# A hybrid decoder layer on one core: the decode sequences of gated linear attention in row and column groups, and decode attention with its two kv heads in turn

## The reference, cut to what matters

```python
    def step(S, xs):
        qd_i, kdec_i, v_i, bl_i = xs
        o_i = jnp.einsum('bhtd,bhde->bhte', qd_i, S)
        S = jnp.exp(bl_i)[:, :, 0, :, None] * S + jnp.einsum('bhsd,bhse->bhde', kdec_i, v_i)
        return S, o_i
```

## Time and profile before

| | before |
|---|---|
| median of three runs | 2471.78 us |
| the profiled execution | 2467.32 us |
| its span | 2465.5 us |
| TensorE busy (weight loads) | 2346.9 us, 95% (2182.4, 89%) |
| VectorE, ScalarE, GpSimd busy | 63%, 37%, 10% |
| mean granted clock of TensorE | 0.983 |
| chain that ended last | TensorE 91%, DMA 3%, VectorE 2%, issue 2%, ScalarE 1% |

### The profile page before, as it was taken

How to read it: one execution, slowest core, us unless ns; L and a number is a source line. 1 busy time by engine, 2 the same in 40 slices (tenths; PEclk the granted TensorE clock), 3 DMA queues, 4 the chain that set the end, 5 groups by cost and what they waited for, 6 DMA issues and landing times.

```text
span 2465.5 us, 44142 instructions
## 1 busy us (share of the span) xinstructions
PE 2346.9 (95%) x18537; PEld 2182.4 (89%) x18537; DVE 1553.5 (63%) x2236; ACT 921.7 (37%) x1324; POOL 238.7 (10%) x285
## 2 busy tenths in 40 slices
PE   5689999999999899899999999999999989999996
PEld 1179888788787799899999999999999989999996
DVE  0342552323232422588888888888888788888898
ACT  2122442323232322544444444444444433333343
POOL 3150140000000111200000000000000211011131
PEclk9989999999999999999999999999999999999998
DMA  9955465555553434214434433443344586365562
GB/s 339 342 184 175 154 157 190 188 181 188 171 192 121 160 110 127 103 69 167 150 123 162 163 118 126 164 166 135 135 167 166 207 301 212 132 228 203 172 212 95
DMA packets 190949, 422.41 MB, mean 171 GB/s; under 512 B 14564, under 2 KB 116756, under 8 KB 188704
## 3 DMA queue, kind: packets, MB, share of 16 engines
q1 hardware_dynamic: 171072, 341.35, 40.4%
q0 software_dynamic: 17088, 73.78, 8.6%
q10 hardware_dynamic: 2592, 4.46, 0.5%
HBM read 365.45 MB, written 54.08 MB: 170 GB/s over the span
## 4 chain that ended last, share of the span: by engine, by line
PE 91%; DMA 3%; DVE 2%; issue 2%; ACT 1%; SPq 0%; POOL 0%; DVEq 0%; POOLq 0%; ACTq 0%
PE PJ L2290 27%; PE PS L2290 27%; PE PJ L1924 25%; DMA AR<-in_weights 3%; PE PJ L1877 2%; PE PJ L1867 1%; PE PJ L2255 1%; PE PS L2150 1%; PE PS L2181 1%; PE PS L2255 1%; PE PS L2174 1%; PE PJ L1889 1%; PE PJ L2232 1%; DVE X L1844 0%; PE PS L2153 0%
## 5 line engine op out<-in xcount | busy, mean ns | idle before, releaser
L2290 PE MATMUL PS<-HS,WO 128*128 128x272 f32 x5376 | 684.2, 289 | 10.3 <-issue 9.5
L2290 PEld LDWEIGHTS PS<-HS,WO 128*128 128x128 f32 x5376 | 679.4, 188 | 11.9 <-issue 11.9
L2290 PE MATMUL PJ<-HS,WO 128*128 128x272 f32 x5376 | 680.6, 288 | 0.0
L2290 PEld LDWEIGHTS PJ<-HS,WO 128*128 128x128 f32 x5376 | 677.3, 188 | 0.0
L1100 ACT ACTIVATE WO<-GR 128x1024 fp32r<-128x1024 f32 (+1 forms) x462 | 477.0, 1033 | 508.5 <-PE PS L2290 243.6
L1619 DVE TENSOR_TENSOR WO<-GR,WO 128x1024 fp32r<-128x1024 f32 (+1 forms) x462 | 556.2, 1204 | 117.6 <-ACT WO L1100 117.5
L1924 PE MATMUL PJ<-HH,WH 128*128 128x272 f32 x1568 | 348.1, 304 | 20.7 <-issue 7.9
L1924 PE MATMUL PJ<-HL,WH 128*128 128x272 f32 x1568 | 327.7, 291 | 0.0
L1924 PE MATMUL PJ<-HH,WL 128*128 128x272 f32 x1568 | 327.5, 291 | 0.0
L1259 DVE TENSOR_TENSOR WL<-RW,WH 128x1024 fp32r<-128x1024 f32 x102 | 129.4, 1273 | 285.5 <-ACT WH L839 285.2
L1924 PEld LDWEIGHTS PJ<-HH,WH 128*128 128x128 f32 x1568 | 248.7, 191 | 55.2 <-issue 43.3
(11 more groups left out here) (308 smaller groups left out, 1846.3 us busy)
## 6 DMA issues: line engine op xcount, KB each, us to landing
GR<-in_weights SPq DMA_DIRECT2D x264, 512.0 KB, 6.7
AR<-in_weights SPq DMA_DIRECT2D x256, 256.0 KB, 4.5
RW<-in_weights SPq DMA_DIRECT2D x102, 512.0 KB, 4.4
HS<-act_parts POOLq DMA_DIRECT2D x91, 544.0 KB, 5.9
act_parts<-SQ SPq DMA_DIRECT2D x40, 952.0 KB, 7.0
AR<-in_weights SPq DMA_DIRECT2D x64, 512.0 KB, 5.3
MIX<-in_xT SPq DMA_DIRECT2D x1, 4352.0 KB, 16.7
X<-in_xT POOLq DMA_DIRECT2D x4, 1088.0 KB, 10.1
```

The costliest lines, as they stand in the source:

```text
L2290: mm = e.matmul(out, w[part], HS[:, HS_AT[QUARTER[i]], y, (2 * first + k) % (KT // 2), :], start=OPENS[i] and k == 0 and x == 0, stop=k == ...
```

## The change

GLA, decode part. A span of 32 tokens that starts at sequence 2j (`windows`, `scol(2 * j)`) is given to column group and row group j = 0 to 3, so its first eight tokens are those of sequences 2j and 2j + 1. `turn_windows` replaces the 32-column transposes of keys and values by four matmuls with the identity into the four partition quarters. `dec_outs`, at k=6 of gg0, makes all decode outputs with 12 matmuls: for each j the masked queries of its two sequences times their states, and ATD times values, into free columns of a PJ bank. ScalarE copies them to OTD (128 rows, of each group the first eight count) in gg0, squares them into OTS with the blocks, and takes the root ahead of the adaLN rows of gg1. `seq_pair(n)`, at k=7, 9, 12 and 14 of gg1, makes two state updates from two row groups, into two PSUM banks. VectorE applies them in the new order; the last four come after the reciprocal and the scaling of OT. KDM is made by two products with a per-row mask DR, which is loaded by four small DMAs on GpSimd ahead of the caches. `o_turn` transposes OTD 128 wide, and `mix_head` picks eight columns of each 32.

Decode attention. `dec_scores` and `dec_values` run the same matmuls in another order: the kv head is the inner loop, so neighbouring matmuls belong to different halves of the array.

```diff
-    KDM = sb("KDM", [32, DEC_B, P], at=en_at)
+    KDM = sb("KDM", [P, 2, P], at=en_at)
...
-    OTD = sb("OTD", [32, DV])
+    OTD = sb("OTD", [P, DV])
...
-    ATD = sb("ATD", [32, 32])
+    ATD = sb("ATD", [P, 64])
...
+    def windows(t):
+x = decode(t)
+return bass.AP(x.tensor, x.offset, [x.ap[0], [2 * DEC_T, 4], [1, 32]], runtime_checks=x.runtime_checks,
+               dep_tracking_offset=x.dep_tracking_offset)
+    def dec_out(m):
+return PJ[:, 2 * (m + 1).mod(2) + 1, DV:2 * DV]
...
+lo, up = CST["dec_rows"]
+for j in range(4):
+    g.dma_start(DR[32 * j:32 * j + 32, :], ins["consts"][0:32, lo:up]).then_inc(S["masks_in"], 16)
...
-        a.activation(GVT[0:32, NB, P * e:P * e + P], PS[0:32, 1, 0:P], ACT.Copy).then_inc(S["gv_by_token"], 1)
+        a.activation(GVT[:, NB, P * e:P * e + P], PS[:, 1, 0:P], ACT.Copy).then_inc(S["gv_by_token"], 1)
...
+    a.wait_ge(S["dec_out_mm"], h + 1)
+    a.activation(OTD[:, :], dec_out(m), ACT.Copy).then_inc(S["out_sq"], 1)
...
+    a.wait_ge(S["out_sq"], (NB + 2) * h + 1)
+    a.activation(OTS[:, :], OTD[:, :], ACT.Square, accum_out=VR[:, 0, NB:NB + 1]).then_inc(S["out_sq"], 1)
+    a.wait_ge(S["out_sq"], (NB + 2) * (h + 1))
+    a.activation(VR[:, 1, :], VR[:, 0, :], ACT.Sqrt, bias=eps, scale=1.0 / DV).then_inc(S["norm_rms"], 1)
...
-    a.wait_ge(S["dec_out_mm"], h + 1)
-    a.activation(OTD[:, :], PS[0:32, 3, 0:DV], ACT.Square, accum_out=VR[0:32, 0, NB:NB + 1])\
-        .then_inc(S["out_sq"], 1)
-    a.wait_ge(S["out_sq"], (NB + 1) * (h + 1))
-    a.activation(VR[:, 1, :], VR[:, 0, :], ACT.Sqrt, bias=eps, scale=1.0 / DV).then_inc(S["norm_rms"], 1)
     a.wait_ge(S["norm_r"], h + 1)
     for b in range(NB // 2):
         a.activation(OT[:, b, :], o_block(b), ACT.Copy, scale=VR[:, 2, b:b + 1]).then_inc(S["out_scaled_a"], 1)
-    a.activation(OTD[:, :], PS[0:32, 3, 0:DV], ACT.Copy, scale=VR[0:32, 2, NB:NB + 1])\
-        .then_inc(S["out_scaled_a"], 1)
+    a.activation(OTD[:, :], OTD[:, :], ACT.Copy, scale=VR[:, 2, NB:NB + 1]).then_inc(S["out_scaled_a"], 1)
...
+        d.scalar_tensor_tensor(out=decode(tile).rearrange("p (j t) -> p j t", j=4),
+                               in0=PS[:, 2, P * e:P * e + P].rearrange("p (j c) -> p j c", j=4)[:, :, 0:8],
+                               scalar=gain, in1=decode(GG[e][:, :]).rearrange("p (j t) -> p j t", j=4),
+                               op0=ALU.mult, op1=ALU.mult)\
...
+    cols = cst("dec_cols")[:, 0:64].rearrange("p (g c) -> p g c", g=2).unsqueeze(2).broadcast_to([P, 2, 4, 32])
+    d.tensor_tensor(QDM[:, :, :].rearrange("p (g j) c -> p g j c", g=2), windows(GQ[:, :]).unsqueeze(1).broadcast_to([P, 2, 4, 32]), cols, ALU.mult)\
+        .then_inc(S["q_by_seq"], 1)
...
+    d.wait_ge(S["masks_in"], 48 + 64)
+    for n in range(2):
+        mm = d.tensor_scalar(KDM[:, n, :], KDT[:, NB, :], DR[:, n:n + 1], None, ALU.mult)
+    mm.then_inc(S["k_by_seq"], 1)
...
-    for b in range(DEC_B):
-        if b == 4:
-            lo(v + (1 + LEAD))
-        if b == 5:
-            head_mod("gg1")
+    def seq_update(x):
+        b = 2 * (x % 4) + x // 4
...
+        d.wait_ge(S["seq_mm"], DEC_B * h + x + 1)
         d.scalar_tensor_tensor(out=SD[:, b, :], in0=SD[:, b, :], scalar=EB[:, last:last + 1],
-                               in1=PS[:, 2, 0:DV], op0=ALU.mult, op1=ALU.add)\
-            .then_inc(S["seq_up"], 1)
-
+                               in1=chunk_up(x), op0=ALU.mult, op1=ALU.add).then_inc(S["seq_up"], 1)
...
+    for b in range(2):
+        seq_update(b)
+    lo(v + (1 + LEAD))
+    for b in range(2, 4):
+        seq_update(b)
+    head_mod("gg1")
...
     d.wait_ge(S["norm_rms"], h + 1)
     d.reciprocal(VR[:, 2, :], VR[:, 1, :]).then_inc(S["norm_r"], 1)
     d.wait_ge(S["norm_r"], h + 1)
     for b in range(NB // 2, NB):
         d.tensor_scalar(OT[:, b, :], o_block(b), VR[:, 2, b:b + 1], None, ALU.mult)\
             .then_inc(S["out_scaled_d"], 1)
+    for b in range(4, DEC_B):
+        seq_update(b)
...
-    for kv in range(KVH):
-        rows = slice(HD * kv, HD * kv + HD)
+    for new in range(2):
         for b in range(DEC_B):
-            out = PS[32 * (b % 4):32 * (b % 4) + 32, kv, 160 * (b // 4):160 * (b // 4) + 160]
-            e.matmul(out[:, 0:WIN], QS[rows, b, :], KC[rows, b, :], start=True, stop=True)
-            mm = e.matmul(out[:, WIN:160], QS[rows, b, :], decode(KTT[rows, :]), start=True, stop=True)
-        mm.then_inc(S["dec_scores"], 1)
+            for kv in range(KVH):
+                rows = slice(HD * kv, HD * kv + HD)
+                out = PS[32 * (b % 4):32 * (b % 4) + 32, kv, 160 * (b // 4):160 * (b // 4) + 160]
+                keys, at = (decode(KTT[rows, :]), slice(WIN, 160)) if new else (KC[rows, b, :], slice(0, WIN))
+                mm = e.matmul(out[:, at], QS[rows, b, :], keys, start=True, stop=True)
+                if new and b == DEC_B - 1:
+                    mm.then_inc(S["dec_scores"], 1)
...
-    for kv in range(KVH):
-        rows = slice(HD * kv, HD * kv + HD)
-        for b in range(DEC_B):
-            n, r = 2 * kv + b // 4, 32 * (b % 4)
-            out = PS[rows, 0, 16 * b:16 * b + 16]
-            e.matmul(out, VC[:, b, rows], PT[0][:, n, r:r + 16], start=True, stop=False)
-            mm = e.matmul(out, VTK[0:32, NB, rows], PTN[:, n, r:r + 16], start=False, stop=True)
+    for b in range(DEC_B):
+        for new in range(2):
+            for kv in range(KVH):
+                rows, n, r = slice(HD * kv, HD * kv + HD), 2 * kv + b // 4, 32 * (b % 4)
+                values, probs = (VTK[0:32, NB, rows], PTN) if new else (VC[:, b, rows], PT[0])
+                mm = e.matmul(PS[rows, 0, 16 * b:16 * b + 16], values, probs[:, n, r:r + 16],
+                              start=not new, stop=bool(new), skip_group_check=True)
     mm.then_inc(S["dec_values"], 1)
...
-        mm = e.transpose(PS[:, 2, 32 * x:32 * x + 32], OTD[:, P * x:P * x + P], ident[0:32, 0:32])
+        mm = e.transpose(PS[:, 2, P * x:P * x + P], OTD[:, P * x:P * x + P], ident)
...
+def turn_windows(t):
+    for j in range(4):
+        at = scol(2 * j)
+        mm = e.matmul(PS[32 * j:32 * j + 32, 1, 0:P], t[:, at:at + 32], ident, start=True, stop=True)
+    return mm
...
-        e.transpose(PS[0:32, 1, 0:P], decode(ED[:, :]), ident).then_inc(S["k_turned"], 1)
+        turn_windows(ED).then_inc(S["k_turned"], 1)
...
-    def sequence(b):
-
-        out = PS[0:32, 3, 0:DV]
-        if b == 0:
+    def dec_outs():
+        out = dec_out(at(h, "gg0")[0])
+        e.wait_ge(S["state_in"], 16 * (h + 1))
+        e.wait_ge(S["q_by_seq"], h + 1)
+        for n in range(3):
+            for j in range(4):
+                x, y = (ATD[:, 2 * DEC_T * j:2 * DEC_T * j + 32], GVT[:, NB, :]) if n == 2 else \
+                    (QDM[:, 4 * n + j, :], SD[:, 2 * j + n, :])
+                mm = e.matmul(out[32 * j:32 * j + 32, :], x, y, start=(n == 0), stop=(n == 2),
+                              skip_group_check=True)
+        mm.then_inc(S["dec_out_mm"], 1)
+    def seq_pair(n):
+        if n == 0:
             e.wait_ge(S["state_up"], NCH * (h + 1))
-            e.wait_ge(S["state_in"], 16 * (h + 1))
             e.wait_ge(S["k_by_seq"], h + 1)
-            e.wait_ge(S["q_by_seq"], h + 1)
-        mm = e.matmul(out, QDM[:, b, :], SD[:, b, :], start=(b == 0), stop=(b == DEC_B - 1))
-        if b == 0:
-            e.matmul(out, ATD[:, :], GVT[0:32, NB, :], start=False, stop=False)
-        if b == DEC_B - 1:
-            mm.then_inc(S["dec_out_mm"], 1)
-        if b:
-            e.wait_ge(S["seq_up"], DEC_B * h + b)
-        e.matmul(PS[:, 2, 0:DV], KDM[:, b, :], GVT[0:32, NB, :], start=True, stop=True)\
-            .then_inc(S["seq_mm"], 1)
-
-    def spread(k, f, ns):
-        return {k + j: [lambda c=c: f(c)] for j, c in enumerate(ns)}
+        else:
+            e.wait_ge(S["seq_up"], DEC_B * h + 2 * n)
+        for x in (2 * n, 2 * n + 1):
+            rows = slice(32 * (x % 4), 32 * (x % 4) + 32)
+            e.matmul(chunk_up(x), KDM[rows, x // 4, :], GVT[rows, NB, :], start=True, stop=True)\
+                .then_inc(S["seq_mm"], 1)
...
-    beside("gg0", 4, 10, {3: [lambda: v_turn(1)]}, *[chunks_of(5 + 2 * n, n) for n in range(6)])
+    beside("gg0", 4, 10, {3: [lambda: v_turn(1)], 6: [dec_outs]}, *[chunks_of(5 + 2 * n, n) for n in range(6)])
     beside("gg1", 5, 10, chunks_of(1, 6), chunks_of(3, 7), {5: [lambda: block_out(NB - 1)]},
-           spread(6, sequence, range(DEC_B)))
+           {k: [lambda n=n: seq_pair(n)] for n, k in enumerate((7, 9, 12, 14))})
```

More of the change, by code:

```diff
@@ L2138, in v_turn @@
                 mm.then_inc(S["gv_turned"], 1)
-                e.transpose(PS[0:32, 1, 0:P], decode(GV[x][:, :]), ident).then_inc(S["gv_turned"], 1)
+                turn_windows(GV[x]).then_inc(S["gv_turned"], 1)
             def pair_up(n):
```

16 lines of the change are left out of this document (5 added, 11 removed).

## The result

The changed kernel took 2440.55 us (median of 4 runs, 2438.74 to 2444.85) beside 2470.85 us of the kernel before (2464.72 to 2472.15): a ratio of 0.9884, 95% interval 0.9872 to 0.9896. Its profiled execution took 2438.74 us, its span 2436.6. Timed once more, with later experiments, it took 2444.94 us (2441.97 to 2446.72) beside 2468.99: 0.9905, interval 0.9890 to 0.9919. By the two timings the change is worth 30.3 and 24.1 us; the forecast was 31.5 us, and 2440 for the median.

What follows compares the result with a forecast made beforehand. TensorE was taken as the bound (busy 95% of the span, 91% of the chain). Terms -26.2 + 5.5 - 1.7 - 2.4 - 1.4 - 5.3 = -31.5 us took the median from 2471.8 to 2440; range 2432 to 2452, forecast's own 2436 to 2445.

Steps and rivals of the forecast that it cites:

- the rule from pair to pair less 0.50: TensorE side job's cost: time from the weight-stream pair before it to the second pair after, less 0.50 us.
- 6.54: GLA heads, sequences: us off per head, 4.96 in place of 11.5; 26.2 us off in four heads.
- The waits costed at nothing: GLA heads, new order: TensorE waits on state updates cost nothing, bound 0 to 1.5 us per head.
- The rival: GLA heads: VectorE paces the pairs, TensorE waits up to 1.5 us per head, total 2446; chance 0.15.
- 2.4 us predicted: Wait before the output projection: norm done earlier, Silu starts as the matmuls end, 2.4 us off.
- The term beside it: Output projection entry: no fall to the lower clock after a 2.1 us idle time, 1.4 us off.
- 5.3 predicted: Decode attention: cost 5.6 us in place of 10.9, lower clock included, 5.3 us off; bounds 0 and 7.
- The term of the values: Decode attention, dec_values: 4.1 us in place of 8.5 with the kv heads in turn.
- The first rival: Decode attention: 16-column products do not overlap, dec_values stays at 8.5 us with its long fall, total 2445; chance 0.12.
- the rival of 2472: Whole change: packing does not act in dec_outs, turns or values, no gain, 2472 us; chance 0.02.
- the seven that would have made it slower: GLA heads: long lower-clock falls of 4.6 us each, seven the deciding point, 2477 us with eight; chance 0.03.
- more gained: No fall after dec_values and 0.3 us less in every turn, total 2435 us; chance 0.13.

Runs made afterwards that it cites:

- the kernel that goes group by group: Changed kernel with the three dec_outs products of each column group behind one another, not in rounds over the groups: 2448.77 us beside 2470.35, ratio 0.9909.
- the last experiment: Changed kernel with DR laid in SC's space, values sorted, window turns directly ahead of the adaLN half products: 2432.33 us beside 2468.99, 0.9854.
- the kernel with the late root and the change's queue: Changed kernel with ScalarE's root only after the sixth update product, VectorE's order as in the change: 2463.75 us beside 2470.35, 0.9968.
- The sorted values: Changed kernel with all decode attention value products of cached keys first, then all of new keys: 2439.20 us beside 2470.35, 0.9870.

## Why the prediction was right, and where not

**The sequences.** Predicted 1.64 us for dec_outs and 0.83 for a pair, by the rule from pair to pair less 0.50: measured 402.64 + 0.36 - 400.87 - 0.50 = 1.63 (the stream's next pair is at 403.00), and 428.30 - 426.97 - 0.50 = 0.83. In the trace's single records four of dec_outs start within 20 ns, and the rounds of four start 0.216 us apart (the first two 0.240), as do the last records of a single group in the kernel that goes group by group: four times, as rows 3 said. The Trainium skill ("TensorE: Matmul & The Clock Gate", "Measured speedup vs the span model") would have given 3.07 times or less; the trace doesn't agree with it for this shape.

**Turns.** 0.46 more was predicted for each. Four transposes and a turn of windows take 395.79 - 394.29 - 0.50 = 1.00 us by the same rule; the five transposes of before took 0.55. So it is 0.45. Of it only about 0.1 are the products; the rest is the change of form, and the last experiment took it back. o_turn: 0.42 predicted (its own rows, 1.46 - 1.07, give 0.39), 0.45 measured (1.46 to 1.01).

**Heads.** 6.54 - 3 x 0.46 + 0.42 = 5.6 a head by the prediction, 5.66 measured. The waits costed at nothing are nothing: no pair waits, gv0's wait is 2.35 where it was 2.33, and not by the QDM product, which takes 0.42 after and 0.43 before; the kernel before with 32 bytes more waits 2.34 and 2.35 too. That this hung on the early root, and what it costs without, the kernel with the late root and the change's queue shows: 4.0 to 6.9 us a head, not the 1.5 that I had as the bound. The rival was well named and under-priced, since the lower clock came behind the wait of 2.46 us in three of the four heads (440.63, 560.10 and 799.03, not in head 2).

**The end of the last head.** 2.4 us predicted, 2.1 as the wait: measured 2.49 and 2.11. The term beside it, 1.4 us for a fall that wouldn't come, failed: the clock fell at 778.59. The step that failed is "an idle time of 2.1 us may be too short for a fall". Over all kernels the clock fell at each of the five waits of 4.60 to 4.70 us, at five of eight waits of 2.11 (leaving out the kernel where another wait lay just ahead), and at 19 of 42 waits of 2.33 to 2.35 ahead of gv0. In the same kernel one head has a fall and the next none. In the same place the fall thus came in all of five long waits and five of eight short ones, so the shorter wait buys some 0.5 us on average by my estimate, and not 1.4. In the whole output projection TensorE was busy at the lower clock for 9.98 us before (three falls) and 8.67 after (two, one of them of 6.83), which is 0.6 us.

**Decode attention.** 5.3 predicted; 5.2 measured between the first scores, and 0.4 behind them, where the long low clock reached before: 5.6. The term of the values was a little large (4.1; 3.56), the fall behind them came as said (3.41 us). The first rival, no overlap of 16-column products, is refuted: 8.52 to 3.56, and at the full clock 0.215 us a product before and 0.111 after. The Trainium skill ("TensorEngine Tiling (Array Packing)", "Instruction Overhead") states some 60 cycles for each matmul and advises against a tiling factor from a dimension that is already small. The factor of two here comes from the 64 columns of the weight tile, and the traces show that products with only 16 moving columns gain it almost in full. The sorted values show what the rest of the time was, 0.106 us for each change between 128 and 32 rows and 0.065 for a product.

**What the sum lacked.** The prediction named DR only for its DMAs. That it moves other tiles by 32 bytes, and that this costs 4.6 us in the feed-forward part, isn't in it, and no row of the kernel before could have shown it. Against it stood gains that weren't in the sum either: 1.5 for a fall in head 3 that only the kernel before had, 1.1 of start, and 0.8 in the output projection beside o_turn, of which 0.6 is the clock as said and the rest its pace (125.28 to 125.00 ns between products, less a wait 0.2 longer; both traces of the changed kernel and the two with DR placed and the values sorted have 125.0, the ten others 125.3, among them some of the same layout, and it stays unexplained). With 0.6 more than forecast in the attention, the heads and the wait together they make 4.0, against 4.6 in the feed-forward part, 0.6 behind it and the 1.4 of the clock: 28.9 in place of 31.5 us by the spans. The forecast of 2440 is thus right term by term for what the change was meant to do, the clock at the last head's end excepted, and right in the total partly by luck; the second timing, 2444.94, lies at the upper end of the forecast's own range of 2436 to 2445.

**The others.** The packing acts, so the rival of 2472 is gone; no fall stood in the heads of the changed kernel's first trace and one in its second, far from the seven that would have made it slower; and of "more gained" nothing came in the first form: the fall behind the values stayed away once they were sorted, and 0.34 us a turn came once the windows stood beside the adaLN halves.

## What to carry to other kernels

Count the changes of array form before the columns: here an entry and exit cost 0.34 us, four fifths of what a product of 256 columns takes alone (0.43), so thin products belong beside others of their form and in rounds over the column groups. When a change adds even a small tile, compare the start-to-start time of a long stream that it doesn't touch, and place it so that the tiles behind it stay where they were. And before moving a result ahead of other work in an engine's queue, ask what that queue does if it comes late: the same order gave 2.5 us with an early root and cost 4.0 to 6.9 us a head with a late one.

## What the runs showed of the hardware that I had not expected

A tile of 32 bytes that nothing touches made a stream of 10752 fp32r products of 272 columns slower by 0.46 ns each (125.65 to 126.11 ns, 4.6 us in all); one of 64 bytes did not (125.48). The lower clock after a wait of 2.1 to 2.5 us comes in some executions of a place and not in others (19 of 42 ahead of gv0), and costs 1.52 us for 3.41 us of it. A product in another column group can start before earlier ones of a busy group (in the kernel that goes group by group six QDM records start before the first ATD record at 406.14, and only four of them stand ahead of it in the program): three products in a row in one group cost twice the time of the round order (2.80 to 1.43 us), not four times.
